# A chunked two-way recurrence on TensorE: wider operands and a new operand layout, 200 products a step in place of 248

## The chip, the cores and the metric

The kernel runs on one core of one Trainium2 chip. The metric is the device time of one execution in microseconds. It computes two two-layer transformer blocks one after the other; the change touches one stage of the second block, which runs twice.

## The reference

What the touched stage computes is the recurrence of `rwkv7_scan`, for 8 heads of width 64, over 768 tokens (256 context, 512 latent), in both directions:

```python
def rwkv7_scan(f, d, s0, reverse):
    def step(state, inp):
        r_t, w_t, k_t, v_t, kk_t, a_t = inp
        sa = jnp.einsum('bhvk,bhk->bhv', state, -kk_t)
        state = (state * w_t[:, :, None, :] + sa[..., None] * (kk_t * a_t)[:, :, None, :]
                 + v_t[..., None] * k_t[:, :, None, :])
        return state, jnp.einsum('bhvk,bhk->bhv', state, r_t)
    ...
    s_last, ys = lax.scan(step, s0, xs, reverse=reverse)
```

All is float32. The rest of the program (modulation, layer norms, feed-forward and attention layers) is the same in both kernels.

## The kernel before, in words

Most of the program are products of 128 x 128 weights with up to 512 columns. The stage `scan_stage` (line 2580) is another kind of work: it is called once for each half of the heads (4 heads, 2 directions, so 8 independent recurrences) between `prepare_stage` and `head_norm_stage` (lines 2409 to 2414).

The 768 tokens are cut in 12 chunks of 64. For a chunk, the products of decayed `a`, `b`, `k` and `r` (each 64 x 64 for a head and direction) give four 64 x 64 matrices, which are masked to be triangular. The inverse of the unit triangular matrix from `a` and `b` is built up in six levels: level 0 is copied in under a mask from the `a b` products, and each of the levels 1 to 5 takes 16 products in `x_t` (half of them transposes by a unit matrix), a copy by ScalarE (`copy_xt`), 8 products in `g_x`, and a masked copy by VectorE (`extend`). Then come the parts that depend on the running state: `z` (from the state and from the chunk), `u` (inverse times z), the new state (`s_products`, then VectorE's `new_state`), and the output (`y_products`, then `add_y`).

Each engine has its order written out by hand. TensorE's is the loop of lines 2945 to 2982: one pass ("step") of it handles the state part of chunk q, the levels 4 and 5 of chunk x = q + 1, the levels 1 to 3 of chunk new = q + 2, and the first products `a_b` of chunk q + 3, interleaved. ScalarE and VectorE have loops of the same shape (lines 2710 and 2804), and semaphores tie them together. GpSimd multiplies `b` and `k` by their decay factors.

How the products lie on the array: a product of 64 rows (the sum) and 64 weight columns takes one quarter of the 128 x 128 array. Which quarter follows from the partitions: the half on which the operands lie gives the rows, the half to which the result goes gives the columns. `spread` (line 2836) and `gather` (line 2842 to 2850) go through all four quarters in turn; `straight` (line 2858) uses only the two on the diagonal. A step has 248 products: `x_t` 5 x 16, `g_x` 5 x 8, `a_b` 16, `z` 16 and `u` 8 on four quarters (160), and `ak_rb` 16, `rk` 8, `b_k_turned` 16, `v_turned` 8, `s_products` 16 and `y_products` 24 on two (88).

The profile gives a line for the helper, not for the caller: L2842 are the products of `a_b`, L2850 those of `x_t` and `u`, L2858 those of `straight`, L2910 `g_x`, L2923 `z`. Each float32 product is two MATMUL and two LDWEIGHTS instructions, so a step has 992 instructions on TensorE. The names of the profile are those of the memory that the tiles lie in: `residual.1` and `gate_rows.1` are areas that are free in this stage (`flat` and `flat2`).

## Time and profile before

| what | value |
|---|---|
| median of 3 runs | 3635.79 us (3632.63 to 3643.98) |
| the profiled execution | 3630.79 us, its span 3629.0 us |
| mean granted TensorE clock | 0.950 of full speed |
| TensorE busy | 3198.3 us (88%) |
| VectorE busy | 2196.5 us (61%) |
| ScalarE busy | 1292.7 us (36%) |
| GpSimd busy | 135.3 us (4%) |
| `scan_stage`, TensorE's first to last product | 1696.6 to 1874.4 us and 1939.1 to 2116.1 us |

The span runs from the first to the last instruction; the profiled execution's own time is 1.8 us more. A matmul counts as busy from its start to its modelled end, and neighbours overlap. "PEld" is TensorE's weight load, which runs beside the matmuls. "issue" as a releaser means that the engine waited for nothing that the profile shows.

### The profile page before, as it was taken

To read this page: it belongs to the slowest core of one execution; us is meant where nothing else is said; L and a number is where in the kernel's file an instruction comes from. 1 tells how busy PE (TensorE), PEld (TensorE's weight loads), DVE (VectorE), ACT (ScalarE), POOL (GpSimd) and SP (SyncE) were. 2 spreads that over 40 slices of the span, in tenths; PEclk is the share of its full clock that TensorE was granted. 3 is DMA by queue.
4 is the path that set the end of the run, shared out by engine and by line. 5 is a ranking of instruction groups with operands and counts; after the bars stand their busy time and mean duration, and the time that the engine had idled before them with its cause. 6 is when DMAs were issued, how large, how long until landed. Compare 5 with 4: busy or idle time off the path is not lost. (4 is left out here: it accounts for less than half of the span.)

```text
span 3629.0 us, 62518 instructions
## 1 busy us (share of the span) xinstructions
PE 3198.3 (88%) x26318; PEld 2588.0 (71%) x26318; DVE 2196.5 (61%) x3916; ACT 1292.7 (36%) x2197; POOL 135.3 (4%) x174
## 2 busy tenths in 40 slices
PE   6989998996999959986776778999999799879999
PEld 5768876655887748855765766887888677668777
DVE  7678866696787774575445436665666326643344
ACT  2243334324333332254324324112232426642243
POOL 0200000200000000001101100000000000000000
PEclk9989999998999979998999998999999899989999
DMA  7524462202334312210000021333233122022321
GB/s 296 168 94 174 186 178 106 71 24 65 128 129 152 130 66 100 72 51 30 5 32 13 4 73 71 122 124 115 105 141 126 47 86 72 1 64 93 84 98 69
DMA packets 64807, 341.60 MB, mean 94 GB/s; under 512 B 15120, under 2 KB 16656, under 8 KB 29072
## 3 DMA queue, kind: packets, MB, share of 16 engines
q1 hardware_dynamic: 61616, 325.77, 25.8%
q0 software_dynamic: 2048, 9.48, 0.7%
q8 instruction: 208, 3.41, 0.4%
q10 hardware_dynamic: 864, 2.36, 0.2%
q14 instruction: 71, 0.58, 0.1%
HBM read 326.80 MB, written 10.79 MB: 93 GB/s over the span
## 5 line engine op out<-in xcount | busy, mean ns | idle before, releaser
L265 DVE TENSOR_TENSOR weight_lo<-weight_ring,weight_hi 128x1024 fp32r<-128x1024 f32 x341 | 423.2, 1242 | 188.8 <-ACT weight_hi L250 183.7
L250 ACT CAST weight_hi<-weight_ring 128x1024 fp32r<-128x1024 f32 x341 | 355.9, 1044 | 166.3 <-PE banks L422 90.9
L420 PE MATMUL banks<-hT_hi.1,weight_hi 128*128 128x512 f32 x896 | 365.4, 408 | 24.8 <-PEq L383 22.8
L422 PE MATMUL banks<-hT_hi.1,weight_lo 128*128 128x512 f32 x896 | 358.3, 400 | 0.0
L421 PE MATMUL banks<-hT_lo.1,weight_hi 128*128 128x512 f32 x896 | 358.3, 400 | 0.0
L420 PEld LDWEIGHTS banks<-hT_hi.1,weight_hi 128*128 128x128 f32 x896 | 171.2, 191 | 68.2 <-issue 25.9
L421 PEld LDWEIGHTS banks<-hT_lo.1,weight_hi 128*128 128x128 f32 x896 | 171.1, 191 | 41.5 <-issue 1.9
L422 PEld LDWEIGHTS banks<-hT_hi.1,weight_lo 128*128 128x128 f32 x896 | 170.7, 190 | 41.8
L420 PE MATMUL banks<-hT_hi.3,weight_hi 128*128 128x512 f32 (+1 forms) x512 | 175.1, 342 | 8.0 <-PEq L383 8.0
L422 PE MATMUL banks<-hT_hi.3,weight_lo 128*128 128x512 f32 (+1 forms) x512 | 173.7, 339 | 0.0
L421 PE MATMUL banks<-hT_lo.3,weight_hi 128*128 128x512 f32 (+1 forms) x512 | 173.6, 339 | 0.0
L319 DVE SCALAR_TENSOR_TENSOR side_sum<-weight_ring,silu_c2.1,side_sum 128x256 f32<-128x256 f32 x336 | 160.5, 478 | 0.0
L319 DVE SCALAR_TENSOR_TENSOR weight_ring<-weight_ring,silu_c2.1 128x256 f32<-128x256 f32 x336 | 160.4, 477 | 0.0
L519 PE MATMUL banks<-weight_hi,left_hi.6 128*128 128x512 f32 x360 | 145.7, 405 | 8.9 <-DVE weight_lo L265 8.9
L522 PE MATMUL banks<-weight_lo,left_hi.6 128*128 128x512 f32 x360 | 142.7, 397 | 0.0
L521 PE MATMUL banks<-weight_hi,left_lo.6 128*128 128x512 f32 x360 | 142.1, 395 | 0.0
L319 DVE SCALAR_TENSOR_TENSOR weight_ring<-weight_ring,silu_c1.1 128x256 f32<-128x256 f32 x280 | 135.6, 484 | 10.5
L420 PE MATMUL banks<-hT_hi.2,weight_hi 128*128 128x256 f32 (+1 forms) x336 | 115.6, 344 | 10.5 <-PEq L383 10.5
L2692 ACT COPY residual.1<-banks 128x512 f32<-128x512 f32 x120 | 70.4, 587 | 144.3 <-PE banks L2850 143.1
L421 PE MATMUL banks<-hT_lo.2,weight_hi 128*128 128x256 f32 (+1 forms) x336 | 114.7, 341 | 0.0
L422 PE MATMUL banks<-hT_hi.2,weight_lo 128*128 128x256 f32 (+1 forms) x336 | 114.5, 341 | 0.0
L420 PEld LDWEIGHTS banks<-hT_hi.3,weight_hi 128*128 128x128 f32 x512 | 97.1, 190 | 19.3 <-issue 8.2
(741 smaller groups left out, 7634.5 us busy)
## 6 DMA issues: line engine op xcount, KB each, us to landing
weight_ring<-ff SPq DMA_DIRECT2D x64, 1024.0 KB, 4.9
weight_ring<-ada SPq DMA_DIRECT2D x48, 1024.0 KB, 4.9
weight_ring<-up SPq DMA_DIRECT2D x44, 1024.0 KB, 6.9
weight_ring<-ada_ffn SPq DMA_DIRECT2D x24, 1024.0 KB, 5.0
weight_ring<-down SPq DMA_DIRECT2D x20, 1024.0 KB, 4.9
weight_ring<-ada_mix SPq DMA_DIRECT2D x16, 1024.0 KB, 4.8
first_blocks.1<-ada_mix SPq DMA_DIRECT2D x8, 1024.0 KB, 12.0
weight_ring<-cv_in SPq DMA_DIRECT2D x8, 1024.0 KB, 4.8
```

Source lines behind the costliest of these rows:

```text
L250: self.nc.scalar.copy(hi, raw).then_inc(self.hi_made, 1)
L265: self.nc.vector.tensor_tensor(lo, raw, hi.bitcast(F32), ALU.subtract).then_inc(self.lo_made, 1)
L319: ins = self.nc.vector.scalar_tensor_tensor(out=to, in0=w[:, k, :], scalar=vec[:, k, v:v + 1], in1=to, op0=ALU.mult, op1=ALU.add)
L420: nc.tensor.matmul(out, w_hi, x_hi, start=first, stop=False)
L421: nc.tensor.matmul(out, w_hi, x_lo, start=False, stop=False)
L422: return nc.tensor.matmul(out, w_lo, x_hi, start=False, stop=last)
L519: one = nc.tensor.matmul(out, xh, hi[:, kk, :], start=(k == 0), stop=False)
L521: nc.tensor.matmul(out, xl, hi[:, kk, :], start=False, stop=False)
L522: last = nc.tensor.matmul(out, xh, lo[:, kk, :], start=False, stop=(k == k_tiles - 1))
L2692: nc.scalar.copy(XT_flat[c % 2], pair(c, X_AT, 4 * CH)).then_inc(xt_copied[c % 2], 1)
```

## The change

The tiles are laid out anew, the products are formed with wider operands where that is possible, and the order of the loops is shifted. In parts:

- **`a` and `r` side by side, `b` and `k` side by side.** `a_b`, `ak_rb` and `rk` (40 products) become `main_products` (8 products, weights 64 rows x 128 columns (b,k), moving 128 columns (a,r)) and `a` (8 products of 64 x 64, for the other orientation of the `a b` matrix). The masks follow: `mask_ak` and `mask_r`, each 512 elements a partition, in place of one of 512 and one of 256.
- **`b` and `k` turned together.** 16 products of 64 x 64 become 8 with 128 weight columns.
- **Sums over 128 rows.** `UV` holds u on one partition half and v on the other, `BKT` the turned b and k likewise, `RR` the masked products with r. `s_products` goes from 16 products to 8 of 128 rows, and the two terms of y from u and v become `y_from_chunk`, 8 products of 128 rows; the term from the state is `y_from_state`, 8 of 64 x 64.
- **`z` in two parts.** `z_from_chunk` and `z_from_state`, 8 each, run at the end of the step ahead of the one that uses them; VectorE's `copy_z` moves with them.
- **Placing.** `x_t`, `g_x` and `u` keep their counts (80, 40 and 8 a step). `v_turned` now goes through all four quarters, `z_from_chunk` and `u` through two. Copies of u and of v by ScalarE become two each, of 64 partitions; the first level's masked copy (`start_extending`) becomes two of 64 partitions.
- **One more pass of the loops**, from q = -3, takes the place of the `a_b(0)` ahead of them.

On TensorE a step has 8 (`main_products`) + 8 (`a`) + 8 (`b_k_turned`) + 8 (`v_turned`) + 80 + 40 + 8 (`u`) + 16 (z) + 8 (`s_products`) + 16 (y) = 200 products. Three of these blocks have another tile shape than 64 x 64: `b_k_turned` and `main_products` (64 x 128), and `s_products` with `y_from_chunk` behind it (128 x 64).

The core of the diff:

```diff
-                    def ak_rb(c):
-                        pe.wait_ge(bk_decayed, 4 * c + 4)
-                        pe.wait_ge(rc_made, 2 * c + 2)
-                        if c >= 1:
-                            pe.wait_ge(masked3, c)
-                        straight(bank(4, 0), [(of(kexp[c % 2]), of(aexp[c % 3]))])
-                        straight(bank(4, 1), [(of(bexp[c % 2]), of(rc[c % 3]))]).then_inc(hh1_made, 1)
+                    def main_products(c, d):
+                        if d == 0:
+                            pe.wait_ge(a_made, 2 * c + 2)
+                            pe.wait_ge(rc_made, 2 * c + 2)
+                            pe.wait_ge(bk_decayed, 4 * c + 4)
+                            if c >= 1:
+                                pe.wait_ge(bk_copied, c)
+                                pe.wait_ge(v_copied, 2 * c)
+                        for f, h in squares:
+                            j = 2 * d + f
+                            last = nc.tensor.matmul(ps[4 + h][:, 2 * j * CH:2 * (j + 1) * CH], both_of(bk_flat[c % 2], h, j), both_of(ar_flat[c % 3], h, j),
+                                                    start=True, stop=True)
...
                     def b_k_turned(c):
-                        if c >= 1:
-                            pe.wait_ge(v_copied, c)
-                        straight(bank(5, 0), [(of(bexp[c % 2]), lambda h, j: unit[h, :])])
-                        straight(bank(5, 1), [(of(kexp[c % 2]), lambda h, j: unit[h, :])]).then_inc(hh2_made, 1)
+                        pe.wait_ge(ak_masked, c + 1)
+                        pe.wait_ge(r_masked, c + 1)
+                        pe.wait_ge(*extended_to(c, 1))
+                        for j in range(4):
+                            for h in range(2):
+                                last = nc.tensor.matmul(bkt_out[:, h, j * CH:(j + 1) * CH], both_of(bk_flat[c % 2], h, j), unit[half[h], :],
+                                                        start=True, stop=True)
...
                     def s_products(c):
-                        pe.wait_ge(u_copied, c + 1)
-                        bt, kt, vt = (of(BKV[c % 3][:, m]) for m in range(3))
-                        straight(state_bank(7), [(bt, of(U)), (kt, vt)]).then_inc(s_made, 1)
+                        pe.wait_ge(u_copied, 2 * c + 2)
+                        for j in range(4):
+                            for h in range(2):
+                                last = nc.tensor.matmul(by_slot(s_out)[half[h], j, :], BKT[c % 3][:, slot(h, j), :], UV[c % 3][:, slot(h, j), :],
+                                                        start=True, stop=True)
...
                         if has_x:
                             x_t(x, 4)
                         if q >= 0:
-                            z(q)
-                        if has_new:
-                            ak_rb(new)
+                            u(q)
+                            y_from_state(q)
                         if has_x:
                             g_x(x, 4)
                         if has_new:
                             x_t(new, 1)
-                        if q >= 0:
-                            u(q)
-                        if has_new:
                             b_k_turned(new)
+                            v_turned(new)
                         if has_x:
                             x_t(x, 5)
                         if has_new:
                             g_x(new, 1)
                         if q >= 0:
                             s_products(q)
+                            y_from_chunk(q)
                         if has_x:
                             g_x(x, 5)
                         if has_new:
                             x_t(new, 2)
-                        if q >= 0:
-                            y_products(q)
+                        if coming < NCH:
+                            main_products(coming, 0)
+                            main_products(coming, 1)
                         if has_new:
                             g_x(new, 2)
-                            rk(new)
-                            v_turned(new)
+                        if has_x:
+                            z_from_chunk(x)
+                        if coming < NCH:
+                            a(coming)
+                        if has_new:
                             x_t(new, 3)
-                        if q + 3 < NCH:
-                            a_b(q + 3)
+                        if has_x:
+                            z_from_state(x)
                         if has_new:
                             g_x(new, 3)
```

TensorE at the end of a step, before: `g_x(new, 2)` (L2910), `rk` and `v_turned` (L2858), `x_t(new, 3)` (L2850), `a_b` (L2842), `g_x(new, 3)`. The count behind x is of products.

```order
L2910 MATMUL banks<-residual.1 64x64 x8
L2858 MATMUL banks<-gate_rows.1,residual.1 64x64 x8
L2858 MATMUL banks<-unit_squares.1,v.2 64x64 x8
L2850 MATMUL banks<-gate_rows.1,residual.1 64x64 x8
L2850 MATMUL banks<-unit_squares.1,gate_rows.1 64x64 x8
L2842 MATMUL banks<-residual.1 64x64 x16
L2910 MATMUL banks<-residual.1 64x64 x8
```

The same place after the change: `main_products` (L2898), `g_x(new, 2)` (L2943), `z_from_chunk` (L2957), `a` (L2880), `x_t(new, 3)` (L2928, L2933), `z_from_state` (L2967), `g_x(new, 3)`.

```order
L2898 MATMUL banks<-residual.1 128x128 x8
L2943 MATMUL banks<-x_t.1 64x64 x8
L2957 MATMUL banks<-residual.1,masked_ak.1 64x64 x8
L2880 MATMUL banks<-residual.1 64x64 x8
L2928 MATMUL banks<-gate_rows.1 64x64 x8
L2933 MATMUL banks<-unit_squares.1,gate_rows.1 64x64 x8
L2967 MATMUL banks<-gate_rows.1,residual.1 64x64 x8
L2943 MATMUL banks<-x_t.1 64x64 x8
```

Between `x_t(new, 3)` and the `g_x(new, 3)` that needs its copy stand now 8 products of z where 16 of `a_b` stood.

TensorE in the middle of a step after the change: `x_t(new, 1)`, `b_k_turned` (L2909), `v_turned` (L2916), `x_t(x, 5)`, `g_x(new, 1)`, `s_products` (L2994), `y_from_chunk` (L3002).

```order
L2928 MATMUL banks<-gate_rows.1 64x64 x8
L2933 MATMUL banks<-unit_squares.1,gate_rows.1 64x64 x8
L2909 MATMUL banks<-unit_squares.1,residual.1 128x64 x8
L2916 MATMUL banks<-unit_squares.1,v.2 64x64 x8
L2928 MATMUL banks<-gate_rows.1 64x64 x8
L2933 MATMUL banks<-unit_squares.1,gate_rows.1 64x64 x8
L2943 MATMUL banks<-x_t.1 64x64 x8
L2994 MATMUL banks<-residual.1 64x64 x8
L3002 MATMUL banks<-masked_r_products.1,residual.1 64x64 x8
```

The shapes are those of the outputs. The 8 rows of `b_k_turned` stand where 16 stood, and `v_turned` has come up behind them from the end of the step.

## Rows read from the trace of the kernel before

**Rows 1.** The page's first part: TensorE's busy time, share, instructions.
```profile
PE 3198.3 (88%) x26318; PEld 2588.0 (71%) x26318; DVE 2196.5 (61%) x3916; ACT 1292.7 (36%) x2197; POOL 135.3 (4%) x174
```

**Rows 2.** Busy time in stretches: both scans, then eight steps in the first.
```profile
core 0: us, PE busy (x) PEld busy (x) DVE busy (x) ACT busy (x) POOL busy (x), PEclk, DMA share, GB/s
1696.55:1874.37 177.82, 139.31 (x5952) 128.92 (x5952) 75.60 (x223) 64.97 (x167) 17.78 (x40) 0.98 0.02 6
1939.07:2116.07 177.00, 137.09 (x5952) 127.03 (x5952) 75.09 (x223) 65.05 (x167) 17.88 (x40) 0.99 0.02 4
...
sum 115.29, PE 90.21 PEld 83.59 DVE 51.00 ACT 44.37 POOL 14.36; mean PE 11.28 PEld 10.45 DVE 6.37 ACT 5.55 POOL 1.79
```

**Rows 3.** Who TensorE waited for in those eight steps, 1724.68 to 1839.97.
```profile
PE banks L2858 <- issue: 7.7, 11, 1.0
PE banks L2850 <- issue: 6.8, 9, 1.3
PE banks L2850 <- DVE gate_rows.1 L2763: 5.6, 12, 0.6
PE banks L2910 <- issue: 2.3, 4, 0.7
PE banks L2910 <- ACT residual.1 L2692: 1.6, 7, 0.2
```

**Rows 4.** TensorE in order of time: where it restarts after idle time "issue".
```profile
1778.77 0.29 PE L2850 MATMUL banks<-gate_rows.1 64*64 64x64 f32 x5 [1.35 <-issue]
1782.52 0.29 PE L2910 MATMUL banks<-residual.1 64*64 64x64 f32 x5 [0.72 <-issue]
1786.26 0.33 PE L2858 MATMUL banks<-unit_squares.1,v.2 64*64 64x64 f32 x5 [0.60 <-issue]
```

**Rows 5.** Busy time in the stretches from one such restart to the next.
```profile
1778.76:1782.51 3.75, 3.03 (x128) 2.89 (x128) 1.20 (x4) 2.05 (x6) 0.00 (x0) 1.00 0.02 4
1782.51:1786.25 3.74, 3.15 (x128) 3.00 (x128) 2.05 (x8) 1.19 (x4) 0.74 (x2) 1.00 0.01 4
```

**Rows 6.** DMA from 1760 to 1800 us: GB/s in 40 slices, and its one queue.
```profile
GB/s 0 16 0 0 16 0 0 0 16 0 0 0 16 0 0 0 16 0 0 16 0 0 0 16 0 0 0 16 0 0 0 16 0 0 16 0 0 0 16 0
...
q8 instruction: 11, 0.18, 1.9%
```

**Rows 7.** TensorE in order of time: blocks of four quarters, of two, and waits.
```profile
1787.85 0.46 PE L2910 MATMUL banks<-residual.1 64*64 64x64 f32 x16 [0.21 <-ACT residual.1 L2692]
1788.88 0.40 PE L2850 MATMUL banks<-gate_rows.1,residual.1 64*64 64x64 f32 x12 [0.56 <-DVE gate_rows.1 L2763]
1790.41 0.65 PE L2858 MATMUL banks<-residual.1 64*64 64x64 f32 x16
1791.58 0.39 PE L2850 MATMUL banks<-gate_rows.1,residual.1 64*64 64x64 f32 x13
```

**Rows 8.** TensorE in an attention stage, in order of time: blocks of three tile shapes.
```profile
3041.61 0.88 PE L2074 MATMUL banks<-identity.1,probs.2 128*128 128x128 f32 x6
3042.42 1.56 PE L2054 MATMUL banks<-qk_c.1 64*128 64x256 f32 x8
...
3044.72 1.53 PE L2084 MATMUL banks<-probs_turned.3,v_c.1 128*64 128x128 f32 x24
3046.18 0.33 PE L2074 MATMUL banks<-identity.1,probs.2 128*128 128x128 f32 x1
```

**Rows 9.** TensorE behind the scan: 128 weight columns, 2 moving columns.
```profile
1878.83 2.84 PE L2420 MATMUL banks<-head_ones.1,residual.1 128*128 128x2 f32 x24
```

**Rows 10.** ScalarE and VectorE on the inverse's path, groups from 1753 to 1768 us.
```profile
L2692 ACT COPY residual.1<-banks 128x512 f32<-128x512 f32 x5 | 2.9, 587 | 6.5 <-PE banks L2850 6.4
L2763 DVE COPY_PREDICATED gate_rows.1<-level_masks.1,banks 128x256 f32<-128x256 uint8 x6 | 2.5, 442 | 4.9 <-PE banks L2910 4.9
L2774 DVE TENSOR_TENSOR masked_products.1<-banks,masks_by_feature.1 128x512 f32<-128x512 f32 x1 | 0.7, 682 | 0.0
L2702 ACT COPY residual.1<-banks 128x256 f32<-128x256 f32 x1 | 0.4, 373 | 2.3 <-PE banks L2858 2.3
```

More of the change, by code:

```diff
@@ L2622, in scan_stage @@
+            zv_made, z_made, z_copied, u_made, u_copied, s_made, y1_made, y2_made = (sem(n) for n in (
+                "z_from_chunk", "z_products", "z_copied", "u_products", "u_copied", "s_products", "y_from_state", "y_from_chunk"))
             s_summed, s_done, y_added = sem("state_summed"), sem("state_decayed"), sem("y_added")
@@ L2628, in tokens @@
                 return slice(chunk(d, c) * CH, (chunk(d, c) + 1) * CH)
-            half = (slice(0, HD), slice(HD, P))
-            squares = [(i, h) for i in range(2) for h in range(2)]
             def pair(c, at, n=2 * CH):
@@ new lines, in copy_v, with copy_u @@
+                    def copy_v(c):
+                        act.wait_ge(v_made, c + 1)
+                        if c >= 3:
+                            act.wait_ge(y2_made, c - 2)
+                        for f in range(2):
+                            to = UV[c % 3][half[f]].rearrange("p (h d f) n -> p h d f n", h=2, d=2)[:, :, :, f, :]
+                            nc.scalar.copy(to, v_out[half[f]].rearrange("p h (d n) -> p h d n", d=2)).then_inc(v_copied, 1)
+                    def copy_u(c):
+                        act.wait_ge(u_made, c + 1)
+                        for f in range(2):
+                            to = in_b_half(UV[c % 3], f).rearrange("p (a f) n -> p a f n", f=2)[:, :, f, :]
+                            nc.scalar.copy(to, in_b_half(u_out, f).rearrange("p (a n) -> p a n", a=4)).then_inc(u_copied, 1)
@@ new lines, in start_extending @@
+                    def start_extending(c):
+                        dve.wait_ge(g_init, c + 1)
+                        dve.wait_ge(main_made, c + 1)
+                        for f in range(2):
+                            got = main_out[half[1 - f]].rearrange("p h (d f) m n -> p h d f m n", f=2)[:, :, :, f, 0, :]
+                            mask = level[half[1 - f], 0].unsqueeze(1).broadcast_to([HD, 2, 2, CH])
+                            nc.vector.copy_predicated(in_b_half(G[c % 3], f), mask, got).then_inc(extended[c % 2], 1)
@@ L2897, in x_t @@
+                    def v_turned(c):
+                        for d in range(2):
+                            for f, h in squares:
+                                last = nc.tensor.matmul(v_out[half[f], h, d * CH:(d + 1) * CH], v[half[h], f, tokens(d, c)], unit[half[h], :],
+                                                        start=True, stop=True)
+                        last.then_inc(v_made, 1)
                     def x_t(c, l):
@@ L2927, in u, with y_from_state @@
+                    def y_from_state(c):
+                        for j in range(4):
+                            for h in range(2):
+                                last = nc.tensor.matmul(by_slot(y_out)[half[h], j, :], S[c % 2][half[h], j, :], AR_IN[c % 3][half[h], j, 1, :],
+                                                        start=(j == 0), stop=False)
+                        last.then_inc(y1_made, 1)
                     def u(c):
                         pe.wait_ge(z_copied, c + 1)
-                        pe.wait_ge(extended[c % 2], 6 * (c // 2) + 6)
@@ L2930, in u @@
[L2930 to L2940 removed]
+                        pe.wait_ge(*extended_to(c, 6))
@@ new lines, in u @@
+                        if c >= 1:
+                            pe.wait_ge(u_copied, 2 * c)
+                        for d in range(2):
+                            for h in range(2):
+                                for f in range(2):
+                                    last = nc.tensor.matmul(in_b_half(by_head(u_out), f)[:, h, d, :], in_b_half(G[c % 3], f)[:, h, d, :],
+                                                            in_b_half(Z, f)[:, h, d, :], start=True, stop=True)
+                        last.then_inc(u_made, 1)
@@ new lines, in s_products, with y_from_chunk @@
+                    def s_products(c):
+                        pe.wait_ge(u_copied, 2 * c + 2)
+                        for j in range(4):
+                            for h in range(2):
+                                last = nc.tensor.matmul(by_slot(s_out)[half[h], j, :], BKT[c % 3][:, slot(h, j), :], UV[c % 3][:, slot(h, j), :],
+                                                        start=True, stop=True)
+                        last.then_inc(s_made, 1)
+                    def y_from_chunk(c):
+                        pe.wait_ge(r_masked, c + 1)
+                        for j in range(4):
+                            for h in range(2):
+                                last = nc.tensor.matmul(by_slot(y_out)[half[h], j, :], UV[c % 3][:, slot(h, j), :], RR[:, c % 3, slot(h, j), :],
+                                                        start=False, stop=(j == 3))
+                        last.then_inc(y2_made, 1)
```

324 lines of the change are left out of this document (162 added, 162 removed).

## The prediction

> **What bounds the kernel now.** Read first the page's head: TensorE is busy for 88% of the span [rows 1], so work taken from it can count. Then the busy time in stretches: the two scans take 177.8 and 177.0 us, 355 of 3629 us, and run almost wholly at full clock (0.98 and 0.99) [rows 2]. In the eight steps from 1724.68 to 1839.97 a step takes 115.29 / 8 = 14.4 us, of which TensorE is busy 11.3, VectorE 6.4, ScalarE 5.6, GpSimd 1.8. TensorE sets the pace, but it is idle 3.1 us a step, and the list of waits says for what: 16.8 us "issue" in 24 pieces in the rows shown, 5.6 us for the masked copy of the inverse and 1.6 us for its copy by ScalarE [rows 3]. So the real dependences cost 7.2 / 8 = 0.9 us a step, and something that the profile does not name over 2 us.
>
> What it is can be read in order of time. TensorE restarts after such a piece at 1778.77, 1782.52 and 1786.26, each time in the middle of a block of like products, where no semaphore stands [rows 4]. Between two restarts lie 128 matmuls and 128 weight loads, 256 instructions, and this in 3.75 and 3.74 us though the work differs [rows 5]. In the same time the only DMA is a queue of kind "instruction": 11 packets of 0.18 MB, thus 16 KB each, one in every 3 or 4 slices of 1 us [rows 6]. 
>
> The Trainium skill, page "Runtime: NRT & Kernel Launch", section "Instruction fetch mechanics", knows refills of 16 KiB (256 instructions) but calls the cost of crossing a boundary "mostly hidden". By it the idle pieces would have another cause, and fewer instructions would bring nothing of their own; that is rival 3. Rows 4 and 5 speak against it, with over 2 us of idle time a step at these places.
>
> **The change part by part.**
> *Instructions.* 48 products a step less are 192 instructions: 992 become 800, 3.88 pieces become 3.13. At 3.75 us a piece a step cannot be shorter than 11.7 us (before: 14.5; measured 14.4).
>
> *TensorE's own time.* On four quarters 13 matmuls start within 0.39 - 0.22 = 0.17 us, 14 ns each, so 29 ns for a product of two; on two quarters 16 start within 0.65 - 0.22 = 0.43 us, 57 ns a product [rows 7]. Before: 160 x 0.029 + 88 x 0.057 = 9.6 us a step. After, 144 products go through four quarters (`x_t`, `g_x`, `a`, `v_turned`, `z_from_state`), 4.2 us; 24 of 64 x 64 on two (`u`, `z_from_chunk`, `y_from_state`), 1.4 us. The 16 of 128 rows (`s_products`, `y_from_chunk`) go to two column halves; with 128 moving columns such a block of 24 matmuls takes 1.53 us [rows 8], that is pairs of 109 ns, and 64 moving columns are the 57 ns of the rows above: 0.9 us. The 16 with 128 weight columns are not in the trace with short moving operands. Lower bound: 57 ns, as for 64 weight columns; upper: 128 weight columns with only 2 moving ones start every (2.84 - 0.25) / 23 = 0.113 us [rows 9], so two passes 0.22 us, if the two row halves do not overlap. The nearest row has 64-row operands in another shape that do overlap: 4 of 256 and 4 of 512 moving columns in 1.56 us [rows 8], where one after another at 0.85 ns a column would need 2.6 us. I take 0.11 us a product: 1.8 us. Sum after: 4.2 + 1.4 + 0.9 + 1.8 = 8.3 us, 1.3 less.
>
> *Changes of tile shape.* There are none in the scan now; after it six a step (into and out of `b_k_turned`, `main_products`, and the pair `s_products`, `y_from_chunk`). The attention stage prices them: 6 matmuls of 128 x 128 until the next shape starts take 3042.42 - 3041.61 = 0.81 us, 12 pairs of 128 x 64 take 3046.18 - 3044.72 = 1.46 us [rows 8]. That is 6 s + d = 0.81 and 12 s + d = 1.46: s = 0.108, d = 0.16 us for one change. Six are 0.9 us. Bounds: 0, where TensorE waits there anyway; 0.3, if weight loads ahead are lost as well.
>
> *Waits.* In the inverse's path the copy of 0.587 us and the masked copy of 0.442 us [rows 10] stay, and so do the two waits at the end of a step, 0.21 and 0.56 us as the rows show them [rows 7]. Between `x_t(new, 3)` and `g_x(new, 3)` stand 8 products instead of 16: 0.24 us more wait; `x_t(new, 3)` no longer has the slow `rk` and `v_turned` ahead of it, which are 0.9 us before and not needed there. The first masked copy and `mask_ab` are made before the step's end, so `x_t(new, 1)` finds them ready. I set these against each other at 0.
>
> *Other engines.* VectorE gets one copy of 0.44 more and one mask of 0.68 for one of 0.42: 6.4 becomes 7.1 us. ScalarE has two copies of 0.373 us more [rows 10]: 5.6 becomes 6.3. Both stay far under 11.7, so this costs nothing unless it lies in the state's loop (z, copy, u, copy, new state, z), which gains one copy of 0.37 and comes to some 4 us of a step. GpSimd, 1.8 us a step, works a step ahead. Without that lead each of these would count in full.
>
> *A step.* Own time before: 14.4 less the issue pieces. They are 2.2 us of idle plus the running-out of the last product, about 0.2 us, at 3 to 4 places: some 2.9, so 11.5. After: 11.5 - 1.3 + 0.9 = 11.1 us, in pieces of 3.55 us, just under 3.75. Since a slow piece (two-quarter work and a wait) goes over 3.75 and a fast one cannot make it good, I add 0.1 to the 11.7: **11.8 us a step, 2.6 less.** Thus the rule of pieces and the own time end close together, and the idle pieces nearly vanish.
>
> *The scan.* Nine full steps gain 9 x 2.6 = 23.4 us. The last two, with part of the work, gain some 1.6 together in proportion to their instructions. The start gains nothing, since there the pipeline fills, and loses 0.4: the first products now wait for all four products of GpSimd. That is 24.6 a scan, 49 for two. Against the profiled execution, 3630.8 us, this is 3582; the median of the runs, 3635.8, lies 5 above it. I say **3584 us**.
>
> **The rivals.**
> 1. *Forecast*: instructions set the pace, 3584 us. Its own range: at most all 9 pieces a scan (2304 instructions / 256) are gained at 3.75 us, 34 us a scan, 3567 us or a little less where pieces come faster; at least, with changes of shape at 0.3 us, own time 12.0 and steps of 12.3, 2.1 x 9 + 1 = 20 us a scan, 3595. Chance 0.76.
> 2. *The wide weights do not overlap*: 16 products at 0.22 us instead of 0.11, 1.8 us more. Own time 12.9, a step 13.0: 1.4 x 9 + 1 = 13.6 a scan, 3608 us. For it: no row shows them with 64 moving columns. Against it: the pairs of 64 x 128 in rows 8. Chance 0.12.
> 3. *The idle pieces do not hang on the count* but on time or on something else. Then a step shrinks only with the own time, by 0.4 to 0.6 us: 6 us a scan, 3624 us. For it: the restarts are nearly periodic in time too. Against it: 256 instructions in each stretch [rows 5]. The runtime page's rule leads here. Chance 0.06.
> 4. *Slower: changes of shape drain more than in attention.* Each empties the array between blocks of the inverse, of which every `x_t` waits for a `g_x`. The point of decision is an own time of 14.4: 3.3 us more over six, so 0.55 + 0.15 = 0.7 us a change. At 1 us a change own time is 11.1 + 6 x 0.85 = 16.2, 1.8 us a step more, 20 a scan: 3676 us. Against it: 0.16 us in four places of rows 8. The page "TensorEngine Tiling (Array Packing)", section "Key Properties", of the Trainium skill says that a change of tiling mode drains TensorE, without a price. Chance 0.04.
> 5. *The change does not do what it says*, with more than 4 instructions for a wide product. The order shows blocks of 8, and rows 8 two matmuls for each product of other shapes. 3636 us, chance 0.02.
>
> **How the numbers follow.** The likeliest case gives 3584. Below it the range takes in the full 9 pieces, 3564; above it the second rival with the same spread, 3612; outside are rivals 3 to 5 and the edges of the first two. Less than 0.3% (11 us) is what a measurement of this kernel can hardly tell from no change. Faster by more: the first two and half of the third, 0.9; within: 0.06; slower: 0.04.
>
> **What would show it.** Right: 9600 instructions on TensorE in each scan, a scan of 152 to 154 us, steps of 11.6 to 12, instruction packets still 3.6 to 3.9 us apart, "issue" under 1 us a step, blocks of 8 wide products in 0.9 us, changes of shape near 0.16 us. Wrong: packets further apart than 4 us with idle "issue" still there (rival 3), `main_products` or `b_k_turned` in 1.7 us (rival 2), a gap over 0.5 us at each change (rival 4), or TensorE waiting for `copy_u`, `copy_z` or the masks, which would mean that the state's loop had become the path.

## The result, and the profile after

| what | before | after |
|---|---|---|
| median | 3635.73 us (3632.63 to 3643.98, 4 runs) | 3601.01 us (3597.02 to 3603.19, 4 runs) |
| the profiled execution's span | 3629.0 us | 3598.5 us |
| mean granted TensorE clock | 0.950 | 0.941 |
| first scan, first to last product | 177.8 us | 159.0 us |
| second scan | 177.0 us | 158.9 us |

The ratio is 0.990 with a 95% interval of 0.9881 to 0.9918: faster by 30 to 43 us. Forecast were 3584 us, with a range of 3564 to 3612. So the sign and the range held, and about two thirds of the gain came: 34.7 us between the medians, 30.5 between the profiled spans, where 49 were worked out. One later execution of the changed kernel (in the run "after, second time" below) took 6313 us where the other four took 3593 to 3600; it is left out of every median and ratio.

The page's head and its instruction queue, after (to read beside [rows 1]):

```profile
PE 3195.1 (89%) x24014; PEld 2578.0 (72%) x24014; DVE 2212.7 (61%) x3940; ACT 1311.6 (36%) x2245; POOL 135.0 (4%) x174
...
q8 instruction: 191, 3.13, 0.4%
```

TensorE has 2304 matmuls and as many loads less, and the queue of kind "instruction" 17 packets less than the 208 of before (4608 / 256 = 18). TensorE's busy time hardly fell, by 3.2 us, and the kernel became 30 us shorter all the same. The packets kept their distance, 11 in the 40 us from 1760 us on, as in [rows 6].

Busy time in stretches, after: nine steps of the first scan (from new state to new state), then both scans. Columns as in [rows 2].

```profile
1733.77:1841.10 107.33, 94.24 (x3602) 85.17 (x3600) 61.88 (x177) 56.56 (x147) 14.07 (x32) 1.00 0.02 5
1699.26:1858.21 158.95, 135.24 (x4800) 121.44 (x4800) 82.26 (x233) 74.84 (x193) 19.14 (x44) 0.92 0.02 4
1926.81:2085.66 158.85, 136.12 (x4800) 122.94 (x4800) 82.67 (x235) 74.74 (x193) 19.12 (x44) 0.91 0.02 4
```

A step takes 107.33 / 9 = 11.93 us, and its 7202 / 256 = 28.1 pieces come every 3.82 us. In the steps the granted clock is 1.00, over the whole scan only 0.92 and 0.91, where [rows 2] had 0.98 and 0.99. Most of the missing part lies there.

Who TensorE waited for in the same nine steps (to read beside [rows 3]):

```profile
PE banks L2928 <- DVE gate_rows.1 L2790: 5.1, 9, 0.6
PE banks L2943 <- ACT x_t.1 L2708: 3.7, 8, 0.5
PE banks L2933 <- issue: 1.4, 5, 0.5
PE banks L2898 <- issue: 0.8, 2, 0.4
```

"issue" comes to 3.9 us in nine steps (four shorter rows of it are left out here), where the rows of before had 16.8 in eight. The waits for the masked copy and for ScalarE's copy are 8.8 us in nine steps, 1.0 a step, as before. `copy_u`, `copy_z` and the masks are not among the waits: the state's loop did not become the path.

TensorE in order of time, after, around the new shapes: `main_products`, what follows it, `b_k_turned`, what follows it, `s_products`, `y_from_chunk`.

```profile
1770.75 0.46 PE L2933 MATMUL banks<-unit_squares.1,gate_rows.1 64*64 64x64 f32 x14 [0.49 <-issue]
1771.13 1.16 PE L2898 MATMUL banks<-residual.1 64*128 64x128 f32 x16
1772.22 0.46 PE L2943 MATMUL banks<-x_t.1 64*64 64x64 f32 x16
...
1778.56 1.11 PE L2909 MATMUL banks<-unit_squares.1,residual.1 64*128 64x64 f32 x16
1779.60 0.46 PE L2916 MATMUL banks<-unit_squares.1,v.2 64*64 64x64 f32 x16
...
1780.69 0.69 PE L2994 MATMUL banks<-residual.1 128*64 128x64 f32 x16
1781.21 0.64 PE L3002 MATMUL banks<-masked_r_products.1,residual.1 128*64 128x64 f32 x16
```

From the start of a wide block to the start of the next are 1.09 and 1.04 us for 8 products. The row halves overlap: without that it would be 1.8. Taking the forecast's 0.11 us a product, 0.16 and 0.21 us are left for the change out of the shape; into `main_products` it is 1771.13 - 1770.75 less 14 starts of 14 ns, 0.18 us. These are estimates: they hang on the 0.11 and the 14 ns, and the first product of a block is in them too.

**The start of the scan.** Here the two kernels part. Busy time and granted clock in short stretches (PEclk is the granted clock), before:

```profile
core 0: us, PE busy (x) PEld busy (x) DVE busy (x) ACT busy (x) POOL busy (x), PEclk, DMA share, GB/s
1690.00:1696.50 6.50, 0.00 (x0) 0.00 (x0) 1.25 (x5) 2.76 (x13) 4.77 (x10) 0.50 0.71 221
1696.50:1700.00 3.50, 3.44 (x103) 3.48 (x105) 1.53 (x5) 0.00 (x0) 0.00 (x0) 0.56 0.18 71
1700.00:1705.00 5.00, 3.73 (x178) 3.46 (x177) 2.21 (x8) 3.35 (x10) 0.87 (x3) 1.00 0.02 3
```

and after:

```profile
1695.00:1700.00 5.00, 0.84 (x8) 0.87 (x10) 1.46 (x5) 1.62 (x7) 0.78 (x2) 0.50 0.63 217
1700.00:1705.00 5.00, 4.13 (x72) 3.56 (x70) 2.79 (x7) 0.59 (x1) 0.97 (x3) 0.50 0.01 3
1705.00:1710.00 5.00, 4.42 (x86) 4.00 (x87) 0.83 (x3) 3.33 (x11) 0.46 (x1) 0.50 0.01 3
1710.00:1715.00 5.00, 3.59 (x90) 2.80 (x91) 2.21 (x6) 0.68 (x2) 1.29 (x3) 0.50 0.00 0
1715.00:1720.00 5.00, 4.29 (x96) 3.99 (x96) 1.87 (x5) 1.17 (x2) 0.00 (x0) 0.50 0.01 3
1720.00:1725.00 5.00, 4.71 (x136) 4.22 (x138) 1.27 (x4) 3.73 (x12) 0.46 (x1) 0.63 0.01 3
```

TensorE was idle for 16 us before and 17 us after ahead of the scan, and both start at half clock, 0.50 or 1.2 GHz. Before, some 3 us after the first product the clock is 2.4 GHz. After, it stays at 1.2 for 24 us in the first scan; in the second it is at 1.2 for 22 of the first 26 us, with 3 to 4 us at 2.4 in between (mean over the start 0.64 and 0.68, before 0.95 in both). From the first product to the first new state are 34.5 us in both scans, where before had 28.1 and 27.4.

So per scan (first, second), against before: nine steps -22.1 and -24.0 us, the last two steps and the tail -3.1 and -1.3, the start +6.4 and +7.1. Between the scans the way became 3.9 us longer (64.7 to 68.6), and ahead of the first 2.6 us were lost in which nothing was changed. Together 18.8 + 18.2 - 3.9 - 2.6 = 30.5 us. The last two terms are of one execution of each kernel, and the experiments show below that they vary by as much without the change.

### The profile page after: what moved, and what is told of

The parts are those of the page before. It is cut to its first block and busy times, and to the rows that moved or that the text cites. A ratio compares the mean times of both kernels' runs of the same rounds, so it can differ in the third digit from the quotient of the medians.

```text
span 3598.5 us, 58078 instructions
## 1 busy us (share of the span) xinstructions
PE 3195.1 (89%) x24014; PEld 2578.0 (72%) x24014; DVE 2212.7 (61%) x3940; ACT 1311.6 (36%) x2245; POOL 135.0 (4%) x174
## 3 DMA queue, kind: packets, MB, share of 16 engines
q8 instruction: 191, 3.13, 0.4%
## 5 line engine op out<-in xcount | busy, mean ns | idle before, releaser
L420 PE MATMUL banks<-hT_hi.5,weight_hi 128*128 128x512 f32 x256 | 102.3, 400 | 4.9 <-PEq L383 4.9
## 6 DMA issues: line engine op xcount, KB each, us to landing
first_blocks.1<-ada_mix SPq DMA_DIRECT2D x8, 1024.0 KB, 12.4
```

What stands on the lines that cost most here:

```text
L420: nc.tensor.matmul(out, w_hi, x_hi, start=first, stop=False)
```

## The experiments

The theory: (a) the steps go by TensorE's instructions, one piece of 256 in about 3.75 us; (b) the missing part is the start, because there TensorE runs at half clock. The rivals: the steps shortened because TensorE's own time did; the start is longer by its new order, its wide products or its waits. "Start" is from the first product (idle products not counted) to the first new state, "a step" the mean of the nine steps behind it, both for the first and the second scan of the profiled execution.

| kernel | median us | ratio to before (95%) | start us | a step us |
|---|---|---|---|---|
| after, second time | 3594.90 | 0.9901 (0.9885 to 0.9917) | 34.3, 34.5 | 11.8, 11.9 |
| before_warm | 3628.26 | 0.9998 (0.9989 to 1.0008) | 25.9, 26.7 | 14.8, 14.5 |
| after_warm | 3593.87 | 0.9899 (0.988 to 0.9918) | 33.2, 31.5 | 11.9, 12.0 |
| split_main_bk | 3623.23 | 0.998 (0.9969 to 0.9992) | 29.3, 32.3 | 13.9, 13.7 |
| split_bk | 3597.6 | 0.9912 (0.9896 to 0.9929) | 32.7, 31.6 | 12.2, 12.4 |
| after_fill | 3587.86 | 0.9878 (0.9863 to 0.9894) | 29.1, 28.7 | 11.9, 11.8 |
| mixed_warm | 3587.49 | 0.9878 (0.986 to 0.9897) | 29.5, 29.2 | 12.3, 12.0 |
| fill_only | 3591.01 | 0.9889 (0.9872 to 0.9905) | 29.5, 30.1 | 11.6, 12.0 |
| mixed_only | 3592.28 | 0.9897 (0.9878 to 0.9917) | 29.5, 30.5 | 12.1, 12.3 |
| mixed_fill | 3592.74 | 0.9894 (0.9879 to 0.9909) | 32.1, 30.5 | 12.0, 12.2 |
| wide_fill | 3589.95 | 0.9879 (0.9862 to 0.9895) | 29.2, 29.2 | 12.4, 12.0 |
| wide_tail | 3591.66 | 0.9892 (0.9877 to 0.9907) | 29.2, 29.2 | 12.1, 11.9 |

The medians are from different chips; the ratios compare.

### Do the steps go by the number of instructions?

**split_main_bk** puts both wide blocks back into 64 x 64 products on four quarters: 128 instructions more a step, the same arithmetic, less time on the array, and no change of shape at two of the three blocks. The edit of `main_products`; that of `b_k_turned` stands with split_bk:

```diff
-                        for f, h in squares:
+                        for f in range(2):
                             j = 2 * d + f
-                            last = nc.tensor.matmul(ps[4 + h][:, 2 * j * CH:2 * (j + 1) * CH], both_of(bk_flat[c % 2], h, j), both_of(ar_flat[c % 3], h, j),
-                                                    start=True, stop=True)
+                            for n in range(2):
+                                for m, h in squares:
+                                    last = nc.tensor.matmul(ps[4 + h][half[m], (2 * j + n) * CH:(2 * j + n + 1) * CH], BK[c % 2][half[h], j, m, :],
+                                                            AR_IN[c % 3][half[h], j, n, :], start=True, stop=True)
```

> The changed kernel with the wide products of main_products and b_k_turned cut back to 64 x 64, four quarters in turn: 32 more products (128 instructions) a step and only two changes of tile shape instead of six. Theory 1 (pieces of 256 instructions, one every 3.75 us): 928 / 256 = 3.63 pieces, a step of 13.6 to 13.8 us instead of 11.9, idle issue time back at over 1.5 us a step, and with a faster start some 14 us more a scan: about 3629 us. Rival (TensorE's own time bounds, instructions are free): 1.75 + 0.7 us become 1.4 us, 1.06 us less a step, 3580 us.

The nine steps between new states in its first scan, in busy time and in waits:

```profile
1722.42:1847.95 125.53, 91.05 (x4178) 83.56 (x4175) 62.32 (x177) 56.38 (x147) 14.00 (x32) 0.96 0.02 5
```

```profile
PE banks L2946 <- issue: 5.6, 4, 1.8
PE banks L2931 <- DVE gate_rows.1 L2790: 5.3, 9, 0.7
PE banks L2970 <- issue: 3.7, 3, 1.5
PE banks L3005 <- issue: 3.5, 3, 1.2
```

TensorE is busy for 3 us less than in the changed kernel's nine steps (91.05 against 94.24) and they take 18 us more. Its 8353 instructions are 32.6 pieces of 3.85 us. "issue" is back, 26.3 us in these nine steps with the rows left out here, in pauses of up to 1.8 us. A step of 13.7 to 13.9 us is what the number of instructions says; by its own time it would have become shorter than 11.9. The clock has a small part in it: it is 0.96 here, some 10 us at half clock, which can explain at most 5 of the 18 us, and the rows of "issue" alone grew by 22. Rival 3 falls: the idle pieces hang on the count.

**split_bk** does this to `b_k_turned` alone (32 instructions more, no change of shape there).

```diff
-                                last = nc.tensor.matmul(bkt_out[:, h, j * CH:(j + 1) * CH], both_of(bk_flat[c % 2], h, j), unit[half[h], :],
-                                                        start=True, stop=True)
+                                for m in range(2):
+                                    last = nc.tensor.matmul(bkt_out[half[m], h, j * CH:(j + 1) * CH], BK[c % 2][half[h], j, m, :], unit[half[h], :],
+                                                            start=True, stop=True)
```

> Only b_k_turned cut back to 16 products of 64 x 64 on four quarters: 32 instructions more a step, own time 0.41 us less for the products and 0.35 less for two changes of shape. Theory 1 (pieces): 3.25 pieces instead of 3.13, a step of 12.2 to 12.3 us, 3 us more a scan, less about 2 us in the start at half clock: 3601 to 3605 us. Rival (own time): 0.75 us less a step, 3584 us.

Steps of 12.2 and 12.4 us, 0.3 and 0.4 more for an eighth of a piece, 0.47 by the rule. The start became 2 to 3 us shorter, which paid the steps back: 3597.6 us where 3601 to 3605 were expected. The total says nothing by itself.

### Is it the clock at the start?

**before_warm** and **after_warm** put 18 products ahead of the scan, where TensorE is idle. They compute nothing that is used.

```diff
+                    for n in range(18):
+                        nc.tensor.matmul(ps[3][:, 0:P], ident[:], ident[:], start=True, stop=True)
                     pe.wait_ge(loaded, 64)
```

> The kernel before with the same 18 products ahead of each scan, as the control. By the clock theory there are only 3 to 4 us at half clock to win back in a scan: at most 1.5 us a scan, 3633 us against 3636. If it gained as much as the changed kernel (12 us), the products would help by something other than the start's clock.

> The changed kernel with 18 idle products of 128 x 128 (identity by identity, into a bank that is written anew) on TensorE at the start of each scan, in the 8 us in which it waits for the masks. Theory 1 (the clock): the changed scan starts at half clock for 24 us, where the kernel before had full clock after 4 us; with the products ahead it is at full clock within 5 us of the first product, the time from the first product to the first new state falls from 34.5 to 28 to 29 us, and the kernel from 3601 to about 3589 us. Rival (the extra pass of the loops makes the start longer): the start stays over 33 us and the time at 3601 us, whatever the clock.

In before the start becomes 2.3 and 0.6 us shorter, and the total shows nothing of it (0.9989 to 1.0008; the 3 us that were expected at most lie within that). In the first scan the nine steps take 3.8 us more, in the second 0.8 less. In after both expectations are missed: the start is neither at 28 to 29 us nor unchanged, it gains 1.3 and 3.0 us, and the total gains nothing that the measurement can tell. The stretches of after_warm show why:

```profile
1695.00:1700.00 5.00, 4.28 (x45) 4.00 (x47) 1.46 (x5) 1.62 (x7) 1.15 (x3) 0.88 0.61 235
1700.00:1705.00 5.00, 3.45 (x96) 3.09 (x96) 2.79 (x7) 0.61 (x2) 0.60 (x2) 0.80 0.01 3
1705.00:1710.00 5.00, 4.42 (x92) 3.75 (x84) 1.13 (x4) 3.40 (x11) 1.75 (x4) 0.52 0.00 0
```

The clock rose to full and fell back under the scan's own first blocks. So it is not only the idle time ahead of the scan: this start does not hold the clock even where it is given.

From the first product on, after_warm has the same instructions as the changed kernel; beside the 18 products ahead only the clock differs. The second start of the changed kernel, and both of after_warm:

```profile
1926.71:1961.21 34.50, 29.46 (x798) 26.45 (x800) 14.16 (x38) 14.09 (x39) 5.17 (x12) 0.68 0.01 3
1698.79:1732.03 33.24, 27.63 (x798) 24.81 (x800) 14.14 (x38) 14.08 (x39) 5.17 (x12) 0.74 0.01 3
1926.09:1957.61 31.52, 25.37 (x796) 22.55 (x798) 14.14 (x38) 14.39 (x39) 5.18 (x12) 0.84 0.02 4
```

With the mean clock at 0.68, 0.74 and 0.84 the same start takes 34.5, 33.2 and 31.5 us. (At 0.64, in the changed kernel's first start, it is 34.5 too.) Drawn on to 1.00 that is 28 to 29 us, an estimate. So the clock is a cause of the long start, with some 6 us of it. It is not the whole: before_warm has 1.00 in both starts and takes 25.9 and 26.7 us, 1 to 3 us less than that estimate.

**after_fill** keeps the 18 products and adds others between the blocks of the start (for q < 0), at the places where TensorE waits:

```diff
+                    def fill(q, n=2):
+                        if q < 0:
+                            for _ in range(n):
+                                for m, h in squares:
+                                    nc.tensor.matmul(ps[6 + h][half[m], 6 * CH:8 * CH], unit[half[h], :], ident[half[h], :], start=True, stop=True)
...
                         if has_x:
+                            fill(q)
                             x_t(x, 4)
```

> The changed kernel with the 18 products ahead of each scan, and also with groups of 4 to 12 products of 64 x 64 by 128 columns, whose result nobody reads, at the places of the first passes where TensorE waits (passes q = -3 to -1, banks 6 and 7). Theory (clock): with the start at full clock throughout, it takes 28 to 30 us instead of 34.5 (27 by the layout of the blocks, 1 to 2 us for the idle products that do not fit in the waits), and the kernel is 10 us faster than the changed one, ratio to it 0.997. Rival (the start is long by its chain of copies, the clock adds little, as the 1.3 to 3 us won by the 18 products alone could mean): start over 32 us, the same time as with the 18 products alone.

**mixed_warm** reaches it by another way: the 18 products, and both wide blocks as 64 x 64 products in the chunks of the start alone (`c < 3` and `c < 2`).

> The changed kernel with the 18 products ahead, and main_products and b_k_turned as 64 x 64 products on four quarters for the chunks of the start (0 to 2, and 0 and 1), wide after that. By the piece theory instructions cost nothing in the start, since there are waits, and narrow products are shorter at any clock; by the clock theory the denser start reaches full clock as the kernel before does. Start of 27 to 29 us, steps as in the changed kernel (11.9 us): 12 us faster than the changed kernel. If wide products were the better ones everywhere, the start would stay over 32 us.

Both have a start of about 29 us and run in 0.9878 of before, against 0.9901 for the changed kernel beside them: 7 us less in the medians, where 10 and 12 were expected. The intervals of the ratios overlap, but each of their eight runs (3583.6 to 3591.6 us) is shorter than each of the changed kernel's four (3592.5 to 3600.3). With wide_fill (below, 0.9879) these two are the shortest kernels of the study. Note that after_fill puts 128 more matmuls into each start, work that nobody uses, and gains 5.6 us there. The start and nine steps of after_fill:

```profile
1695.05:1724.12 29.07, 25.94 (x926) 22.77 (x928) 14.15 (x38) 14.08 (x39) 5.20 (x12) 0.94 0.01 4
1724.12:1831.55 107.43, 93.32 (x3602) 84.72 (x3598) 61.92 (x178) 56.20 (x147) 14.15 (x32) 1.00 0.02 5
```

and those of the changed kernel:

```profile
1699.16:1733.67 34.51, 29.63 (x798) 26.55 (x800) 14.16 (x39) 14.10 (x39) 5.18 (x12) 0.64 0.01 3
1733.67:1841.00 107.33, 94.24 (x3602) 85.17 (x3598) 61.88 (x178) 56.58 (x147) 14.07 (x32) 1.00 0.02 5
```

In the first scan the nine steps are the same to 0.1 us; the start alone differs, with its clock at 0.94 instead of 0.64.

### Which part of the cure counts, and do they add?

**fill_only** has the fillings without the 18 products, **mixed_only** the 64 x 64 blocks without them, **mixed_fill** all three.

> The changed kernel with the filling products between the start's blocks, but without the 18 products ahead of the scan: only the second half of the edit that gave 28.7 to 29.1 us from the first product to the first new_state and 3587.9 us. If the clock in the start hangs on how densely TensorE works in the start itself, the filling alone brings most of it: the first 3 to 5 us stay at half clock, then it rises; start 30 to 31.5 us, time 3588 to 3592 us. If a start at full clock is only kept and not reached from low (the products ahead are what counts), the start stays at 33 to 34.5 us and the time near 3596 us.

> The changed kernel with both wide blocks in 64 x 64 products on four quarters for the chunks of the start alone (main_products for c < 3, b_k_turned for c < 2), without the 18 products ahead. It has 96 more instructions in the first pieces and 6 changes of shape less in the start. By the theory of the clock (the start is thin in instructions, so the clock stays low) more but shorter products alone give part: the start comes down from 34.5 to 31 to 33 us and the time to 3590 to 3594 us. The rival, that the wide products themselves drain or hold the start and the clock has nothing to do with it, would give the whole gain of the kernel that had the products ahead as well: a start of 29 to 29.5 us and 3587 us, with the clock low all the same.

> Both cures at once: 18 products ahead of the scan, filling products between the start's blocks, and 64 x 64 products in place of the wide ones in the start. Each of the two kernels before it (filled; mixed) has a start near 29 us, where the clock is full for all but some 5 us. If only the clock was the loss, it is bounded by the start at full clock of before (27.4 to 28.1 us): start 27.5 to 29 us, time 3584 to 3587 us, hardly better than either. If the wide products cost the start something beside the clock, the two add: start 25 to 27 us, time 3580 to 3583 us.

fill_only came about as expected (29.5 and 30.1 us, 3591 us). In mixed_only the edit adds 176 matmuls and as many weight loads to a start (974 instead of 798), more than the 96 instructions that the expectation has. It had a shorter start than expected (29.5 and 30.5 us), as its rival said. The clock has a part in it: it is full from 1702 us on, as the stretches show.

```profile
1695.00:1700.00 5.00, 3.34 (x107) 2.98 (x108) 3.21 (x10) 1.64 (x4) 0.00 (x0) 0.50 0.01 3
1700.00:1705.00 5.00, 3.94 (x176) 3.59 (x172) 1.77 (x5) 2.96 (x10) 1.77 (x4) 0.81 0.02 3
1705.00:1710.00 5.00, 3.38 (x184) 3.03 (x184) 2.84 (x8) 2.39 (x5) 0.00 (x0) 1.00 0.01 3
```

The rival has a part in it as well: over the whole start mixed_only's clock is 0.84 and 0.85, what after_warm had in its second scan with 31.5 us. At the same clock the start with the narrow products is 1 to 2 us shorter.

mixed_fill missed both expectations: though its clock is nearly full it has the longest start of the kernels from after_fill on.

```profile
1691.59:1723.73 32.14, 25.45 (x1102) 22.49 (x1104) 14.15 (x38) 14.10 (x39) 5.18 (x12) 0.95 0.02 4
1916.05:1946.55 30.50, 23.97 (x1102) 20.95 (x1104) 14.24 (x38) 14.00 (x39) 5.21 (x12) 1.00 0.02 5
```

2206 instructions are 8.6 pieces, at 3.54 to 3.73 us each: nearly the rule of the steps, in the start. The waits of its first start say the same: 3.8 us "issue" in four rows, of which this is the largest, where wide_fill below has 0.5.

```profile
PE banks L2945 <- issue: 2.4, 2, 1.5
```

The first start of before is near it as well, 1940 instructions, 7.6 pieces, 28.1 us, 3.71 each. But at full clock, in before_warm, the same pieces come every 3.4 and 3.5 us: in a start the rule is no hard bound. That before_warm gained nothing because its scan is bound by the pieces fits its first scan; it is not shown.

**wide_fill** puts the filling into fewer instructions, one product of 128 x 128 for each four.

```diff
-                                for m, h in squares:
-                                    nc.tensor.matmul(ps[6 + h][half[m], 6 * CH:8 * CH], unit[half[h], :], ident[half[h], :], start=True, stop=True)
+                                nc.tensor.matmul(ps[7][:, 6 * CH:8 * CH], ident[:], ident[:], start=True, stop=True)
```

> The filled kernel (18 products ahead, fillings between the start's blocks) with each filling of four quarters, 8 matmuls, replaced by one of 128 x 128 with 128 columns, 2 matmuls: as long at work, with 96 matmuls and 96 weight loads less in a scan. The starts at full clock seen so far have 924 to 1102 matmuls to the first new_state and take 28.7 to 32.1 us, 3.5 to 4.2 us for 256 instructions; the longest has the most of them. If such a start is bound by the number of instructions again, this one, with 830 matmuls (6.5 pieces, 24.3 us at 3.75), comes to 25 to 28 us, and the time to 0.986 to 0.9875 of before. The rival, that a full-clock start is bound by its waits (inverse, masks), leaves it at 28.5 to 29.5 us and the time where the filled kernel was, 0.9878; the 128 x 128 shape may cost it a change of shape at each filling, 0.16 us, about 1 us in all.

```profile
1694.40:1723.63 29.23, 26.53 (x831) 23.15 (x832) 14.15 (x39) 14.00 (x39) 5.17 (x12) 1.00 0.01 3
1919.86:1949.09 29.23, 26.53 (x830) 23.15 (x832) 14.15 (x38) 13.99 (x39) 5.19 (x12) 1.00 0.02 4
```

The rival was right: at full clock throughout and with only 6.5 pieces the start is 29.23 us, in both scans to the hundredth. So this order of work needs about 29 us at full clock with the fillings in it. How much less it would be at full clock without any filling was not measured, since without it the clock falls; after_warm's estimate is 28 to 29 us.

**wide_tail** adds 17 such products in the last two steps of each scan. (The expectation says 25; the edit makes 8 in the last step but one and 9 in the last, and the trace has 34 matmuls of them a scan.)

> wide_fill and 25 more such products (0.22 us each at full clock) in the last two steps of each scan, where TensorE waits for ScalarE and VectorE, so that the stage behind the scan begins at full clock. In the changed kernel that stage's products between 1860 and 1872 us ran partly at half clock and the way from scan to scan was 3.9 us longer than before. If the thin last steps are the cause, the granted clock behind the scan is 1.00 as in the kernel before, and the time is 2 to 5 us under wide_fill's (once, or for both scans). If the cause is the stage's own idle gap of 2 us behind the scan, or the phase in which the clock is looked at, nothing changes beyond 1 us; where the fillings delay u, new_state or z they cost up to 1 us a scan.

The first products behind the first scan, in the changed kernel, in wide_tail, and in the changed kernel's second run, after_again:

```profile
1860.13 4.51 PE L3077 MATMUL banks<-y.1,head_ones.1 128*128 128x512 f32 x8 [2.02 <-PEq L383]
```

```profile
1851.99 2.82 PE L3100 MATMUL banks<-y.1,head_ones.1 128*128 128x512 f32 x8 [0.94 <-PEq L383]
```

```profile
1857.64 2.82 PE L3077 MATMUL banks<-y.1,head_ones.1 128*128 128x512 f32 x8 [1.63 <-PEq L383]
```

The same products take 4.51, 2.82 and 2.82 us. With the fillings the clock is 1.00 there behind both scans, as the theory says. But the changed kernel itself has 2.82 us behind three of its four traced scans, so the slow block does not belong to its thin end; in those three the clock fell in the last step instead (0.66 to 0.67 over its last 5 us). The way from scan to scan says the same: 64.7 us in before, 68.2 in before_warm, 68.6 and 66.6 in the two executions of the changed kernel, 66.3 in wide_tail. And the fillings delayed the state's loop: the last two steps took 18.0 us instead of 15.3, and nothing was left of the gain.

**The changed kernel once more**, beside three of these:

> The changed kernel as it is, on the chip and beside the runs of the two that follow, as their yardstick. Every theory: 0.990 of the kernel before, start (first product to first new state) 34 to 35 us, steps of 11.9 us.

It came as expected. In its first start the clock rose for 3 to 4 us in the middle (mean 0.68) and the start is 34.3 us all the same.

## Why the prediction was right, and where it was not

- **What bounds the scan: right.** Pieces of 256 instructions set the pace, every 3.82 us after the change (forecast 3.6 to 3.9), and split_main_bk shows that it is the count. The Trainium skill, page "Runtime: NRT & Kernel Launch", section "Instruction fetch mechanics", calls the crossing of such a boundary "mostly hidden". The runs disagree: it cost over 2 us a step before and 2.9 us in split_main_bk (26.3 us in nine steps).
- **The step: right, 0.13 us too low.** 11.93 and 11.95 us, forecast 11.8 within 11.6 to 12. 3.13 pieces at 3.82 instead of 3.75 us give it, 1.2 us a scan. Of the forecast gain only 0.7 us are missing for both scans, since the steps of before in the second scan were 14.6 and not 14.4.
- **TensorE's own time: right.** 11.93 less 0.43 of "issue" and, counted as in the prediction, 0.2 us of running-out at each of the 12 pauses in nine steps, is 11.2, forecast 11.1. The wide products overlap (rival 2 falls), and a change of shape costs 0.16 to 0.21 us by the estimate above where 0.16 was taken (rival 4 falls). The Trainium skill, page "TensorEngine Tiling (Array Packing)", section "Key Properties", says that a change of tiling mode drains TensorE. The trace agrees with a pause at each change, and this is its price here.
- **Waits at 0: right.** 1.0 us a step after, 0.9 before.
- **The last two steps: better than forecast** in the first scan, 3.1 us for 1.6, and as forecast in the second, 1.3.
- **The step that failed: "the start gains nothing, since there the pipeline fills, and loses 0.4".** It lost 6.4 and 7.1 us. The working counted instructions and waits there and took the clock as given, though the stretch ahead of the scan is idle and the clock was read at 0.98 over the whole scan, in which the low part is hidden. After the change the clock over the start is 0.64 and 0.68. With the same instructions and 0.84 in after_warm the start is 31.5 us, and after_fill, mixed_warm, fill_only and mixed_only, with 0.84 to 1.00, have 28.7 to 30.5. Against the forecast this is 12.7 us for both scans, of 18.7 that are missing (49.2 less 30.5). A smaller part, 1 to 3 us a scan by the estimate under after_warm, stays at full clock; mixed_only points at the wide products for 1 to 2 us, the rest is open.
- **What was not in the sum at all:** the stage between the scans, 3.9 us, of which 3.3 us are TensorE's products from L3077 to the last of L3084, 14.6 us at a clock of 0.7 to 0.86 where before took 11.3 at 1.00; and 2.6 us ahead of the first scan, where nothing was changed. Both are of one execution: over the fourteen traces the way between the scans is 64.7 to 71.3 us and the first product lies at 1691.6 to 1699.2 us. The kernel before has 64.7 and, as before_warm, 68.2. I take them for scatter; for the 3.9 us that is not fully shown. The missing part of the spans closes: 12.7 (starts) + 3.9 + 2.6 + 0.7 (steps) - 1.2 (last steps) = 18.7 us. Of the medians only 14.5 us are missing (49.2 less 34.7), and the three terms of the scans give 12.2 of them.
- **The range held, partly by luck.** The forecast's own range in rival 1 was 3567 to 3595, and 3601 lies outside it: the start was missing there. The total is inside 3564 to 3612 only by the room that was left for wide weights that do not overlap, and they do overlap. The last line of the sum has a slip as well: with the median 5 us above the profiled execution, 49.2 us less is 3587, not 3584.

What stays open: why the changed start does not bring the clock up while that of before does. The runs show that more products or narrower ones in the same places do it; they do not show why.

## What to carry to other kernels

Where a stage is made of hundreds of small products, count TensorE's instructions and look at the spacing of the "instruction" packets: if TensorE pauses in the middle of a block every 256 instructions, wider operands can pay even if they keep the array busier, as here (94.2 us busy in nine steps and 18 us less than with the narrow products). Then read the granted clock of the first 10 us behind every idle stretch by itself, not as a mean: a change that makes the start of a stage sparser can lose there what it gains later, and a few products that nobody uses, put where TensorE waits, can be cheaper than half the clock. They cost instructions too, so they stop paying where these bound the stage.

## What the runs showed of the hardware that was not expected

- Products whose result nobody uses made the kernel faster: 128 matmuls more in a start and 18 products ahead of it, and the start 5.4 and 5.8 us shorter.
- A start at full clock is no longer bounded by one thing: 29.2 us with 830 matmuls (waits and fillings), 30.5 to 32.1 with 1102 (pieces).
- With the same 18 products ahead of each scan the start of before became 2.3 and 0.6 us shorter and its time stayed the same (before_warm, ratio 0.9998).
- The same 8 products behind a scan took 2.82 us in one execution of a kernel and 4.51 in another, by where the clock fell.
- Products of 64 rows and 128 weight columns on the two row halves overlap: 8 of them and the change out of their shape in 1.04 to 1.09 us.
